# A two-block network in one kernel: the last layer norm by halves of the tokens, and three orders of issue changed

## The reference

```
# first block
h = rms_norm(x) * (1 + sc1) + sh1           # sh1, sc1, gt1, sh2, sc2, gt2 = silu(c) @ w_mod + b_mod
y = concat(chunked_sgu, rg_lru, rwkv7)(h @ w_in) @ w_out
x = x + gt1 * y
h = rms_norm(x) * (1 + sc2) + sh2
x = rms_norm(x + gt2 * conv_glu_ffn(h))
# second block
mix = concat(s5_mixer, retention)(x @ w_in_2) @ w_out_2
x = layer_norm(ALPHA * x + mix, ln1_g, ln1_b)
ffn = (silu(causal_conv3(x @ w_gate)) * (x @ w_val)) @ w_down    # 2816 hidden features
x = layer_norm(ALPHA * x + ffn, ln2_g, ln2_b)                    # the output
```

## Time and profile before

| | us |
|---|---|
| median of three runs | 2649.42 |
| the profiled execution | 2650.58 |
| its span, from first to last instruction | 2648.8 |
| TensorE busy | 2470.6 (93%) |
| VectorE, ScalarE, GpSimd busy | 1428.7, 875.9, 878.8 |
| TensorE's mean granted clock | 0.962 of full |

### The profile page before, as it was taken

How to read it: one execution, slowest core, us unless ns; L and a number is a source line. 1 busy time by engine, 2 the same in 40 slices (tenths; PEclk the granted TensorE clock), 3 DMA queues, 4 the chain that set the end, 5 groups by cost and what they waited for, 6 DMA issues and landing times.

```text
span 2648.8 us, 36791 instructions
## 1 busy us (share of the span) xinstructions
PE 2470.6 (93%) x15003; PEld 1453.8 (55%) x15164; DVE 1428.7 (54%) x1697; ACT 875.9 (33%) x1082; POOL 878.8 (33%) x494
## 2 busy tenths in 40 slices
PE   4899999999889999999998989999889999999996
PEld 1555558886445555555554655575345555555552
DVE  5774666663486640566314863355486640566413
ACT  3245422221144430355313223321155430354303
POOL 0212110000236532455314887001236532455320
PEclk7899999999999999999998999989999999999998
DMA  8511020000301123111322512300111123211311
GB/s 324 231 48 41 21 108 3 3 3 16 119 9 64 48 91 121 67 64 48 120 76 99 112 57 80 120 1 24 56 72 58 55 87 117 75 64 48 118 33 64
DMA packets 53496, 196.29 MB, mean 74 GB/s; under 512 B 5584, under 2 KB 15312, under 8 KB 50384
## 3 DMA queue, kind: packets, MB, share of 16 engines
q1 hardware_dynamic: 45552, 176.38, 19.5%
q10 hardware_dynamic: 7776, 17.56, 1.9%
HBM read 164.55 MB, written 29.36 MB: 73 GB/s over the span
## 4 chain that ended last, share of the span: by engine, by line
PE 77%; DVE 12%; POOL 5%; issue 2%; ACT 2%; DMA 2%; ACTq 0%; SPq 0%; DVEq 0%; POOLq 0%
PE pt L1138 16%; PE pt L1144 15%; PE pt L1141 15%; PE pt L1689 8%; PE pt L573 7%; PE pt L411 3%; PE pt L714 2%; PE pt L2402 2%; PE pt L2408 2%; PE pt L2405 2%; DVE work L536 1%; PE pt L344 1%; DMA work<-in_w_mod 1%; PE pt L332 1%; POOL work L1630 1%
## 5 line engine op out<-in xcount | busy, mean ns | idle before, releaser
L1088 POOL TENSOR_TENSOR slots<-work,weights_rounded 128x512 bf16<-128x512 f32 (+2 forms) x234 | 420.5, 1797 | 598.4 <-ACT weights_rounded L1247 309.2
L1141 PE MATMUL pt<-work,weights_rounded 128*128 128x512 bf16 x1208 | 327.7, 385 | 2.2
L1138 PE MATMUL pt<-rounded,weights_rounded 128*128 128x512 f32 x624 | 210.0, 453 | 15.8 <-POOL slots L1088 10.2
L1138 PE MATMUL pt<-rhs_rounded,weights_rounded 128*128 128x512 f32 x624 | 210.2, 453 | 12.2 <-POOL slots L1088 8.0
L573 PE MATMUL pt<-work 64*64 64x64 f32 (+5 forms) x4512 | 210.7, 243 | 6.6 <-DVE work L536 5.5
L1138 PE MATMUL pt<-hidden_rounded,weights_rounded 128*128 128x512 f32 x704 | 207.2, 427 | 0.3
L573 PEld LDWEIGHTS pt<-work 64*64 64x64 f32 (+3 forms) x4512 | 191.5, 140 | 26.1 <-DVE work L536 7.7
L1141 PEld LDWEIGHTS pt<-work,weights_rounded 128*128 128x128 bf16 x1248 | 100.1, 99 | 168.9 <-issue 98.0
L1144 PE MATMUL pt<-hidden_rounded,slots 128*128 128x512 bf16 x694 | 178.6, 387 | 1.1
L1144 PE MATMUL pt<-rounded,slots 128*128 128x512 bf16 x607 | 168.9, 391 | 1.4 <-issue 0.2
L1144 PE MATMUL pt<-rhs_rounded,slots 128*128 128x512 bf16 x607 | 168.0, 389 | 1.4 <-issue 0.2
(11 more groups left out here) (368 smaller groups left out, 4074.5 us busy)
## 6 DMA issues: line engine op xcount, KB each, us to landing
work<-in_w_up SPq DMA_DIRECT2D x64, 512.0 KB, 4.0
work<-in_w_down SPq DMA_DIRECT2D x32, 704.0 KB, 4.1
work<-in_w_mod SPq DMA_DIRECT2D x10, 2048.0 KB, 8.8
slots<-in_w_in SPq DMA_DIRECT2D x31, 512.0 KB, 3.6
slots<-in_w_up SPq DMA_DIRECT2D x24, 512.0 KB, 4.8
x_scratch<-work ACTq DMA_DIRECT2D x16, 512.0 KB, 2.6
work<-x_scratch SPq DMA_DIRECT2D x16, 512.0 KB, 8.0
slots<-in_w_v SPq DMA_DIRECT2D x10, 512.0 KB, 4.2
```

The costliest lines, as they stand in the source:

```text
L1088: did(pool, pool.tensor_tensor(dst, raw, high.bitcast(F32), ALU.subtract), name)
L1138: pe.matmul(out, whi[:, k * P:k * P + P], rhs_hi(k), start=first and k == ks[0], stop=False, skip_group_check=True)
L1141: pe.matmul(out, top_half(whi)[:, k * P:k * P + P], rhs_lo(k), start=False, stop=False, skip_group_check=True)
```

## The change

Four parts, of which the first is the large one.

1. **The last layer norm by halves of the tokens.** In the second down projection of the second feed-forward the output tiles m = 0, 1, 2 are made as before. The other five are made in ten units of one token half each: u = 0 to 4 are m = 3 to 7 for tokens 0 to 511, u = 5 to 9 the same for 512 to 1023. The five weight tiles are loaded, rounded and split once more for the second half. Between the units stands the norm of the first half: TensorE's mean after unit 5, squares after 6, columns after 7, rows after 8. After unit 9 follows the norm of the second half, and all its operations are 512 wide.
2. **Loads of the first phase.** `load(3)` goes ahead of `load_mod(0)`, and each later `load_mod(g)` stands behind `load(g+2)`, where `load_mod(2)` and `(3)` stood ahead of `load(4)` and each later `load_mod(g)` behind `load(g)`.
3. **GpSimd in the second mixer.** It waits for the same coefficients under another semaphore name; the low part of job 9 stands between `outputs_in(1)` and `outputs_through(1)` rather than ahead of both; `inputs(2)` and `inputs(3)` stand behind the first low part in the items V0 and V1 (jobs 11 and 16) rather than at B.
4. **ScalarE at the first fast tile of each feed-forward.** T1 and block 3 (S1) are rounded ahead of the silu of tile 1, block 4 behind it.

Four semaphores of the S5 set-up are merged into `act_once` and `dve_once`, with the same order of events. The diff, cut to its core:

```diff
@@ -324 +324 @@
+        BOTH = 3
+        SHARE = 8 - BOTH
+        HALF = {"pe": ["lm", "lv", "lc", "rl"]}
+        HALF["act"] = [("lsq", k) for k in range(8)] + ["row", "lroot"] + [("bias", k) for k in range(8)]
+        HALF["dve"] = [("xsum", k) for k in range(BOTH, 8)] + [("cent", k) for k in range(8)] + ["lrecip"] + [
+            ("lns", k) for k in range(8)]
+        def half_wait(eng, who, what):
+            eng.wait_ge(E(f"half_{who}"), HALF[who].index(what) + 1)
+        def half_did(eng, ins, who, what):
+            assert did(eng, ins, f"half_{who}") == HALF[who].index(what) + 1
@@ -1009 +1023 @@
+        def end_bank(b):
+            return PT[(FFN_PT[1] + b // 2) % 4][:, (b % 2) * 512:(b % 2) * 512 + 512]
+        def share_bank(u):
+            return end_bank(u if u < 8 else 4 + u % 4)
+        def share_of(u):
+            return u // SHARE, BOTH + u % SHARE
@@ -1042 +1066 @@
                     sp.wait_ge(E("ffn_w_split"), fast_job(t, half, FH - 2 + m, 6) + 1)
-                sp.dma_start(down_raw(m), down[m, :, half * WCOLS:(half + 1) * WCOLS]).then_inc(E(f"ffn_w_in{n % 4}"), 16)
+                sp.dma_start(down_raw(m), down[m if m < 8 else m - SHARE, :, half * WCOLS:(half + 1) * WCOLS]).then_inc(E(f"ffn_w_in{n % 4}"), 16)
@@ -1080 +1104 @@
                 sp.dma_start(w(XB[t] + m), kept_x(t, m)).then_inc(E(f"x_load{m // 4}"), 16)
-            for m in range(4, 8):
+            for m in range(4, 8 + SHARE * t):
@@ -1119 +1143 @@
                         fast(half, j, p)
-                for m in range(8):
+                for m in range(8 + SHARE * t * half):
-        def ffn_pe(pe, t):
+        def ffn_pe(pe, t, later=None):
@@ -1214 +1238 @@
                     fast(half, j)
-                for m in range(8):
+                for m in range(BOTH if t and half else 8):
                     down(half, m)
+            for u in range(2 * SHARE * t):
+                h, m = share_of(u)
+                pe.wait_ge(E("ffn_w_split"), down_job(t, 1, BOTH + u) + 1)
+                if u < 6:
+                    pe.wait_ge(E("ffn_added"), 16 * t + 8 + u // 2 + 1)
+                elif u >= 8:
+                    pe.wait_ge(E("ffn_added"), 16 * t + 8 + BOTH + u - 4 + 1)
+                at = down_at(BOTH + u)
+                ins = passes(share_bank(u), flat_hi(at, WCOLS), flat_lo(at, WCOLS), range(FH), lambda k: HH[:, k, half_of(h)],
+                             lambda k: hidden_lo(k)[:, half_of(h)], True, True)
+                ins.then_inc(E("ffn_w_used"), 1)
+                if u in later:
+                    later[u]()
-        def ffn_act(act, t, cw, cb):
+        def ffn_act(act, t, cw, cb, later=None):
@@ -1283 +1320 @@
             high(0, PLAIN, (0, 1, 2))
+            t_part("T1")
+            high(0, PLAIN, (3,))
             silu(0, 1)
-            t_part("T1")
-            high(0, PLAIN, (3, 4))
+            high(0, PLAIN, (4,))
@@ -1312 +1350 @@
                 hidden(half, FH - 1)
-                for m in range(2, 8):
+                for m in range(2, BOTH + 2 if t and half else 8):
-        def ffn_dve(dve, t, cw, gain, alpha):
+            for u in range(2 * SHARE * t):
+                if u < 2 * SHARE - 2:
+                    high_down(1, BOTH + u + 2)
+                later(act, u)
+        def ffn_dve(dve, t, cw, gain, alpha, later=None):
@@ -1470 +1512 @@
                 low(half, FH - 1)
-                for m in range(8):
+                for m in range(BOTH if t and half else 8):
                 add_square(dve, SQF, 16, 7)
+            for u in range(2 * SHARE * t):
+                h, m = share_of(u)
+                dve.wait_ge(E("ffn_w_used"), down_job(t, 1, BOTH + u) + 1)
+                dve.wait_ge(E(f"x_load{m // 4}"), 128 * (t + 1))
+                xm = w(XB[t] + m)[:, half_of(h)]
+                did(dve, dve.tensor_tensor(xm, xm, share_bank(u), ALU.add), "ffn_added")
+                later(dve, u)
@@ -1591 +1640 @@
             ffn_sp(sp, 1, a["w_up_2"], a["w_down_2"])
-            for k in range(8):
-                sp.wait_ge(E("x4_ready"), k + 1)
-                sp.dma_start(a["out"][:, k, :], w(H + k)).then_inc(E("out"), 16)
-            sp.wait_ge(E("out"), 128)
+            for h in range(2):
+                for k in range(8):
+                    if h:
+                        sp.wait_ge(E("x4_ready"), k + 1)
+                    else:
+                        half_wait(sp, "act", ("bias", k))
+                    sp.dma_start(a["out"][:, k, half_of(h)], w(H + k)[:, half_of(h)]).then_inc(E("out"), 16)
+            sp.wait_ge(E("out"), 256)
@@ -1669 +1718 @@
                     for n in jobs_of(it):
-                        split_lo(n + 3)
+                        if it != "k0":
+                            split_lo(n + 3)
+                        if it[0] == "V" and n == jobs_of(it)[0]:
+                            inputs(int(it[1]) + 2)
                     if it == "u2":
-                        pool.wait_ge(E("s5_coefs"), 1)
+                        pool.wait_ge(E("dve_once"), 5)
                         outputs_through(0)
-                elif it[0] == "B" and it[1] < 3:
-                    inputs(it[1] + 1)
+                elif it[0] == "B" and it[1] == 0:
+                    inputs(1)
                 elif it[0] == "C" and it[1] < 3:
-                    outputs(it[1] + 1)
+                    outputs_in(it[1] + 1)
+                    if it[1] == 0:
+                        split_lo(job2["k0"] + 3)
+                    outputs_through(it[1] + 1)
@@ -1932 +1987 @@
+            def mean(h):
+                if h:
+                    pe.wait_ge(E("ffn_added"), 24 + BOTH + 2 * SHARE)
+                    pe.wait_ge(E("x_sums"), 14)
+                else:
+                    half_wait(pe, "dve", ("xsum", 7))
+                pe.matmul(end_bank(4 * h), const("ones"), w(XSUM[1])[:, half_of(h)], start=True, stop=True,
+                          skip_group_check=True).then_inc(E("pt_filled" if h else "half_pe"), 1)
+            def squares(h):
+                for k in range(8):
+                    if h:
+                        pe.wait_ge(E("squares"), 32 + k + 1)
+                    else:
+                        half_wait(pe, "act", ("lsq", k))
+                    ins = pe.matmul(end_bank(4 * h + 1)[0:1, :], const("ones")[:, 0:1], w(k)[:, half_of(h)], start=(k == 0),
+                                    stop=(k == 7), skip_group_check=True)
+                ins.then_inc(E("pt_filled" if h else "half_pe"), 1)
...
+            ffn_pe(pe, 1, {5: lambda: mean(0), 6: lambda: squares(0), 7: lambda: columns(0), 8: lambda: rows(0)})
+            mean(1)
+            squares(1)
+            columns(1)
+            rows(1)
         def mixer2_act(act):
             def A_(dst, src, func, name, **kw):
@@ -2070 +2166 @@
...
+            def end_act(act, n):
+                if n == 5:
+                    squares(0)
+                if n == 6:
+                    kept_row(0)
+                if n == 7:
+                    root(0)
+                if n in (8, 9):
+                    biased(0, range(4 * (n - 8), 4 * (n - 8) + 4))
+                if n == 9:
+                    squares(1)
+                    kept_row(1)
+                    root(1)
+                    biased(1, range(8))
+            ffn_act(act, 1, "ffn_conv_w_2", "ffn_conv_b_2", end_act)
         def mixer2_dve(dve):
             def V_(ins, name="dve_step"):
                 return did(dve, ins, name)
             c = s5c
-            dve.wait_ge(E("s5_dt"), 1)
+            dve.wait_ge(E("act_once"), 4)
             V_(dve.tensor_tensor(c(XRE), c(LRE), c(DTC), ALU.mult))
             V_(dve.tensor_tensor(c(TURN), c(LIM), c(DTC), ALU.mult))
@@ -2303 +2459 @@
...
+            def total(h, k):
+                acc = w(XSUM[1])[:, half_of(h)]
+                ins = dve.tensor_tensor(acc, acc, w(H + k)[:, half_of(h)], ALU.add)
+                if h:
+                    V_(ins, "x_sums")
+                else:
+                    half_did(dve, ins, "dve", ("xsum", k))
+            def centered(h):
+                filled(dve, "lm2") if h else half_wait(dve, "pe", "lm")
                 for k in range(8):
-                    V_(dve.scalar_tensor_tensor(w(H + k), pt(f"lm{t}")[:, :], -1.0 / D, w(H + k), ALU.mult, ALU.add),
-                       "centered" if k < 7 else "pt_emptied_dve")
-                rstd_dve(dve, f"lc{t}", 1.0 / D, LN_EPS)
-                filled(dve, f"rl{t}")
+                    xk = w(H + k)[:, half_of(h)]
+                    ins = dve.scalar_tensor_tensor(xk, end_bank(4 * h), -1.0 / D, xk, ALU.mult, ALU.add)
+                    if h == 0:
+                        half_did(dve, ins, "dve", ("cent", k))
+                    else:
+                        V_(ins, "centered" if k < 7 else "pt_emptied_dve")
...
+            def end_dve(dve, u):
+                h, m = share_of(u)
+                total(h, m)
+                if u == 5:
```

(18 more changed lines are left out.)

162 lines of the change are left out of this document (115 added, 47 removed).

## The result

The changed kernel takes 2605.51 us, the median of four runs (2600.56 to 2608.22), against 2651.04 beside it: a ratio of 0.9834, with a 95% interval of 0.9818 to 0.985, or 40 to 48 us less. The forecast was 2606.1, the sum 43.3. The profiled execution, at 2600.56, is the lowest of the four; its span is 2598.8. The two spans differ by 50.0 us, the medians by 45.5. What that scatter is, the experiments show.

The account below looks back on a forecast made before the run. TensorE, busy 93% of the span, bounds the kernel, so edits pay where it waits or another engine works alone behind it. 9.0 + 8.3 + 15.6 + 10.4 = 43.3 us off 2649.4 gives 2606.1; forecast 2598 to 2613 (0.60).

Parts of the forecast that it names:

- Tail: Last down projection and layer norm by token halves: 26.8 us exposed for 47.9, 12.1 more between units; gain 9.0, 6 to 12.
- The bound of 3 us: Covered norm between the tail's units: its 12.1 us may run faster, by up to 3, at a better clock.
- The cover of 1.9 us: Tail units: weights' rounding and low part take 5.5 of 7.4 us, leaving 1.9 before units run late.
- Loads: First phase: weight loads ahead of modulation loads bring VectorE sooner to its second convolution; gain 8.3 us, 5 to 13.7.
- GpSimd: Second mixer: value weights ahead of coefficients remove waits worth 19.5 us, add 3.9; gain 15.6, 8 to 19.5.
- The first two places: Second mixer: S5 output tables ahead of tile 9's split, 4.8 us; first value block's last low part ahead of coefficients, 7.8.
- Rival (b): Second mixer: GpSimd's chain bounds it, 4 us late in both rounds; 2614 to 2620 with a low tail; 0.20 with (c).
- T1 and S1: First fast tiles of both feed-forwards: rounding ahead of the silu starts TensorE sooner, 5.2 us each; 10.4, 7 to 13.
- (c): Tail: low parts of 6.5 us stretch ten units by 1 us each, the tail gains nothing; 2615; 0.20 with (b).
- (d): Tail: TensorE's clock falls to 1.2 GHz from unit 6 and stays, costing 53 us; 2659; chance 0.04.
- (a): Low parts do not hold VectorE up, or TensorE's clock gives more back; 2594 to 2598; chance 0.12.
- (e): Whole kernel: no change within 0.2%, a chain handing every gain on to a later wait; chance 0.04.

Follow-up runs that it names:

- changed: The changed kernel with all four parts, against the kernel before: 2605.51 us, ratio 0.9834.
- changed_again: The changed kernel itself measured a second time, nothing altered, against the kernel before: 2598.84 us, ratio 0.9812.
- gpsimd_only: The kernel before with only GpSimd's new order of low parts and S5 coefficients in the second mixer: 2638.24 us, 11.4 us gain.
- round_only: The kernel before with only ScalarE's new order at the first fast tile of both feed-forwards: 2642.58 us, 6.4 us gain.
- loads_only: The kernel before with only the new order of loads in the first phase: 2639.27 us, 8.5 us gain.

## Why the prediction was right

The measured time, 2605.5 us, is 0.6 from the forecast 2606.1, and each of the four mechanisms was found in the trace. That it comes so close is in part luck. The four executions spread over 7.7 us, and the terms were off by 0.4 to 2.9 us in changed, by 1.0 to 4.3 in changed_again: 9.0 + 8.3 + 15.6 + 10.4 = 43.3 was the sum, 11.9 + 9.6 + 15.2 + 11.4 = 48.1 are the bold fields of changed, and 13.3 + 9.5 + 13.1 + 9.4 = 45.3 those of the same kernel in changed_again. The other fields of changed, -1.1, -4.5, -0.1 and +3.8, bring its sum to 50.0; fields of that size stand in kernels without an edit there. By the ratio the gain is 44. Point by point:

**Tail.** 11.9 us and not 9.0, inside 6 to 12. The exposed norm was 26.1 for 26.8, step by step within 0.8 us: add to mean 2.9 (forecast 2.6), centring and square 1.5 (1.5), squares 8.4 (7.8), row to reciprocal 2.3 (2.9), root 0.3 (0.35), rows 1.3 (2.0), scalings 6.2 (6.0), bias and transfer 3.3 (3.6). The mis-sized term is the covered norm: 12.1 us in the prediction, 9.2 measured (0.45 + 6.96 + 0.98 + 0.81, each from its start to the start of the next unit). It was taken as half of the exposed tail of before, where the clock was 0.89 in the squares, 0.65 in the columns and 0.50 in the rows; between the units it was 1.00. The mean had the full clock in both, and gains because the next unit starts 0.45 us behind it, before its 1.02 us are over. The bound of 3 us was the right size for both together. With the units' own 0.7 us the last unit ends 9.9 us later. The cover of 1.9 us was about right: the first of GpSimd's nine low parts there takes 3.99 us and ends 1.4 ahead of its unit, the others take 3.2 and end 2.2 or more ahead.

The table load of 1.28 us stands under unit 8 in changed, and the root follows it within 0.01 us:

```profile
2557.86 1.28 ACT L2216 ACT_TABLE_LOAD   x1 [0.53 <-DVE small L2502]
2559.15 0.21 ACT L2216 ACTIVATE small<-small 128x4 f32<-128x4 f32 x1
```
By the Trainium skill (ScalarE: Activation LUTs, What ACT_TABLE_LOAD costs) a drain of some 1.4 us belongs to the switch. No row here shows one: the load starts 0.1 us after the reciprocal that it waits for has ended (2557.78). That the tail gave 11.9 and not 9.0 is no sign of it, since the covered norm is where that difference arose.

**Loads.** Each count was right: three more products of 3.27 us (five for two), one wait of 2.30, the convolution at 129.8 for the forecast 131. 8.3 alone, 9.6 in changed.

**GpSimd.** The first two places gave 12.3 us in gpsimd_only (12.6 forecast): the 48 matmuls of S5 behind the first value block start at 1562.0 where they started at 1580.1, 18.1 us sooner, of which 5.8 were there at 1490. The new waits were 1.7, 1.8 and 1.3, together 4.8 for 3.9: tile 17 was 1.2 later than said, as the coefficients ahead of it take 17.2 us (1582.6 to 1599.8) and not the 16.0 of the earlier trace rows, probably because they now stand beside more of VectorE's work. Rival (b) named this chain rightly, but it cost 1 us, not 4.

**T1 and S1.** The waits became 3.1 and 4.8 us. The step that the prediction did not have is the wait of 1.7 us for VectorE in the first feed-forward: its sums of 0.69 us take 1.6 to 1.8 beside GpSimd's low parts. The executions without it gain no more for that (round_only), since there the matmuls behind the wait for T1 run at the lower level of the clock, as they do in the kernel before. Before and after:

```profile
795.80 2.07 PE L1138 MATMUL pt<-rhs_rounded,weights_rounded 128*128 128x512 f32 x4 [8.04 <-POOL slots L1088]
```

```profile
775.54 1.19 PE L1162 MATMUL pt<-rhs_rounded,weights_rounded 128*128 128x512 f32 x4 [3.10 <-POOL slots L1112]
```

**Rivals.** (c) fell with the cover, (d) with the clock of 1.00 in the covered squares. (a)'s first mechanism, no cost of a meeting, fell: the products show the cost five times. What it had right was the tail, where the clock and the overlap with the units gave 2.9 us. (e) fell.

## What to carry to other kernels

Price a step that moves under other work at the clock and duration of the place where it goes, not of the one that it leaves. When two engines' queues are reordered, count which operations will now run side by side, and add the length of each meeting. When a change's parts lie hundreds of us apart, compare the same instruction's start in both traces stretch by stretch; it tells a gain of 5 us where the timed medians can't, and shows which differences no edit can have made. Do it in more than one execution: one kernel's stretches differed here by up to 3 us, and a single trace flatters or hides an edit by as much.

## What the runs showed of the hardware

- A two-source product on VectorE (1.23 us) was held 2.04 us by a GpSimd subtraction of 2.46 us and 0.86 us by a GpSimd copy of 1.04 us; it ended 1.1 us after each.
- Executions differ in TensorE's granted clock over the same instructions: 0.98 or 0.99 over the recurrences, 4.5 us. Kernels that share no edit can show the same difference: -1.7, -1.6 and -1.6 us in the stretch to 382 in gpsimd_only, round_only and loads_only.
- The same sixteen float32 matmuls of the exposed squares took 7.0, 8.3 and 9.9 us in three executions, at a granted clock of 1.00, 0.84 and 0.71.
- Summing eight 512-wide squares to one row took TensorE 7.0 us in float32 and 2.0 in float32r, both at the full clock.
